# A hybrid decoder trunk's state-space scan: decay differences and six output gates on GpSimd, norm weights in the weight splits, z gates one step earlier

## What is computed

```python
zxbcdt = h @ w_in                                   # 1024 -> 2048 z, 3072 x/B/C, 32 dt
xbc = silu(causal_depthwise_conv(xbc, conv_w, conv_b))
a_cs = cumsum(dt * a)                               # per chunk of 128 tokens and head
decay = exp(where(causal, a_cs[l] - a_cs[s], -inf)) # 128 x 128 per head
y = (C B^T * decay) @ (x * dt) + (C @ state) * exp(a_cs) + d_skip * x
y = rms_norm(y * silu(z), norm_w)                   # norm_w: one weight per channel of 2048
x = x + g1 * (y @ w_out)                            # g1: the layer's output gate, from c
```

## Time and profile before

| | |
|---|---|
| median of 3 runs | 1495.35 us (1494.41 to 1498.49) |
| the profiled execution | 1497.73 us, its span 1495.9 us |
| PE busy, share of the span | 96% |
| DVE busy | 67% |
| ACT busy | 50% |
| POOL busy | 1% |
| granted PE clock | 0.991 |
| DMA, mean | 338 GB/s |

### The profile page before, as it was taken

How to read it: one execution, slowest core, us unless ns; L and a number is a source line. 1 busy time by engine, 2 the same in 40 slices (tenths; PEclk the granted TensorE clock), 3 DMA queues, 4 the chain that set the end, 5 groups by cost and what they waited for, 6 DMA issues and landing times.

```text
span 1495.9 us, 18527 instructions
## 1 busy us (share of the span) xinstructions
PE 1437.1 (96%) x6840; PEld 976.6 (65%) x6840; DVE 995.1 (67%) x1271; ACT 747.6 (50%) x977; POOL 18.6 (1%) x27
## 2 busy tenths in 40 slices
PE   7989999999999899999999999999999989999998
PEld 2835787888789778674666556756465655565573
DVE  2578788888659899764666646765654555655563
ACT  3565544444455896353446445644453444545361
POOL 0000000000000000000100000000000000000000
PEclk9999999999999999999999999999999999999999
DMA  9878698888366545679999999999999999999996
GB/s 361 330 248 292 240 396 303 301 295 301 103 217 185 162 161 204 261 288 409 364 412 406 411 374 416 418 420 420 409 420 413 420 420 418 413 420 414 420 419 247
DMA packets 118201, 506.01 MB, mean 338 GB/s; under 512 B 13779, under 2 KB 16492, under 8 KB 83032
## 3 DMA queue, kind: packets, MB, share of 16 engines
q1 hardware_dynamic: 115640, 496.51, 85.6%
q0 software_dynamic: 2464, 8.24, 1.6%
HBM read 502.52 MB, written 2.32 MB: 337 GB/s over the span
## 4 chain that ended last, share of the span: by engine, by line
PE 74%; DVE 10%; DMA 7%; ACT 6%; issue 3%; SPq 0%; DVEq 0%; ACTq 0%
PE acc L2685 16%; PE acc L2693 16%; PE acc L2686 16%; PE acc L3187 15%; DVE w_lo L1581 3%; ACT w_hi L1038 2%; DVE cv L2308 2%; DMA raw_rest<-in_moe_w_down 1%; DMA raw<-in_moe_w_down 1%; PE xb L3071 1%; DMA mod<-in_moe_w_gu 1%; PE acc L2834 1%; DMA mod<-in_moe_w_down 1%; DMA raw<-in_ada_w 1%; ACT dec L1487 1%
## 5 line engine op out<-in xcount | busy, mean ns | idle before, releaser
L1581 DVE TENSOR_TENSOR w_lo<-raw,w_hi 128x1024 fp32r<-128x1024 f32 x356 | 427.3, 1221 | 136.6 <-ACT w_hi L1038 126.1
L1038 ACT ACTIVATE w_hi<-raw 128x1024 fp32r<-128x1024 f32 x356 | 371.0, 1057 | 249.1 <-PE acc L2693 157.7
L2685 PE MATMUL acc<-w_hi,g_hi 128*128 128x512 f32 x448 | 179.3, 400 | 4.0 <-ACT w_hi L1038 3.9
L2686 PE MATMUL acc<-w_hi,g_lo 128*128 128x512 f32 x448 | 174.8, 390 | 0.0
L2685 PE MATMUL acc<-w_hi,a_hi 128*128 128x512 f32 x384 | 155.4, 405 | 8.5 <-ACT z_s L1404 7.7
L2686 PE MATMUL acc<-w_hi,a_lo 128*128 128x512 f32 x384 | 151.4, 394 | 0.0
L2693 PE MATMUL acc<-w_lo,g_hi 128*128 128x512 f32 x448 | 139.1, 392 | 4.1 <-DVE w_lo L1581 4.1
L3187 PE MATMUL acc<-raw,g_s 128*64 128x512 f32 x592 | 131.6, 594 | 0.5 <-DMA raw<-in_moe_w_gu 0.5
L2693 PE MATMUL acc<-w_lo,a_hi 128*128 128x512 f32 x384 | 119.5, 392 | 0.0
L1581 DVE TENSOR_TENSOR w_lo<-mod,w_hi 128x1024 fp32r<-128x1024 f32 x66 | 78.5, 1221 | 60.0 <-ACT w_hi L1038 58.2
L2685 PEld LDWEIGHTS acc<-w_hi,g_hi 128*128 128x128 f32 x448 | 84.2, 188 | 38.4 <-issue 12.7
(11 more groups left out here) (417 smaller groups left out, 2057.3 us busy)
## 6 DMA issues: line engine op xcount, KB each, us to landing
raw<-in_moe_w_gu SPq DMA_DIRECT2D x136, 1024.0 KB, 14.8
raw<-in_moe_w_down SPq DMA_DIRECT2D x66, 1024.0 KB, 16.5
raw<-in_ada_w SPq DMA_DIRECT2D x96, 512.0 KB, 6.0
mod<-in_moe_w_gu SPq DMA_DIRECT2D x40, 1024.0 KB, 13.8
raw<-in_ffn_w_gu SPq DMA_DIRECT2D x56, 512.0 KB, 5.9
mod<-in_moe_w_down SPq DMA_DIRECT2D x23, 1024.0 KB, 16.3
raw_more<-in_moe_w_gu SPq DMA_DIRECT2D x22, 1024.0 KB, 14.3
raw<-in_ssm_w_in SPq DMA_DIRECT2D x40, 512.0 KB, 5.0
```

Of the source, the lines that this page charges most:

```text
L1038: act.activation(w_hi[:, w % SPLIT, :], raw_tile(no), ACT.Copy).then_inc(hi_ready, 1)
L1581: dve.tensor_tensor(w_lo[:, w % SPLIT, :], raw_tile(no), r32(w_hi[:, w % SPLIT, :]), ALU.subtract).then_inc(raw_used, 1)
L2685: pe.matmul(o, l_hi[:, k, rows_], hi[:, col:col + HALF], start=new, stop=False)
L2686: pe.matmul(o, l_lo[:, k, rows_], hi[:, col:col + HALF], start=False, stop=False)
```

## The change

Three things are done.

1. **Decay differences on POOL.** POOL's loop over the units, which issued the loads of `acs_in`, now also computes the differences: eight `tensor_scalar` of 128x128 per unit, subtract and then minimum with 0. ACT's eight Relu go, and its Exp has no scale of -1 now. `acs_used` is set by POOL, and ACT waits for it.
2. **The output gate of six tiles on POOL.** After its differences of units 4, 5 and 6 POOL multiplies two `wout` tiles each by the gate row (`tensor_tensor`, 128x1024). DVE's `GATED_AT` goes. `y_gain` goes out of the gate and into the splits: for the 16 `wout` tiles ACT's split is an Identity with a scale per partition in place of a Copy, and DVE's a `scalar_tensor_tensor` in place of a `tensor_tensor`. DVE's ten other gates become `tensor_tensor`.
3. **z one step earlier.** `z_of_group(j)` stands at step `PROJ_END[Z0 + j] + 1`, that is 28, 32, 36 and 40, and ahead of the unit's Exp.

```diff
 def gated_no(stage, i):
-    return i + 1 + (KD if stage == "wout" else 0)
+    return i + 1 + (KD - GATED_AHEAD if stage == "wout" else 0)
...
 # ACT, split_hi
-act.activation(w_hi[:, w % SPLIT, :], raw_tile(no), ACT.Copy).then_inc(hi_ready, 1)
+if in_wout(no):
+    k = no - raw0["wout"]
+    act.activation(w_hi[:, w % SPLIT, :], raw_tile(no), ACT.Identity, scale=y_gain[:, k:k + 1]).then_inc(hi_ready, 1)
+else:
+    act.activation(w_hi[:, w % SPLIT, :], raw_tile(no), ACT.Copy).then_inc(hi_ready, 1)
...
 # ACT, gemm
-act.wait_ge(gated, gated_no(stage, i))
+if i < GATED_AHEAD:
+    act.wait_ge(gated_ahead, i + 1)
+else:
+    act.wait_ge(gated, gated_no(stage, i))
...
 # ACT, mixer_steps
+for j in range(SG):
+    if i == PROJ_END[Z0 + j] + 1:
+        z_of_group(j)
 for u in range(NU):
     if i == unit_in_at(u) + LEAD:
         unit_decays(u)
 if i in DECAYS_FIRST:
     conv_silu(i)
-for j in range(SG):
-    if i == PROJ_END[Z0 + j] + 2:
-        z_of_group(j)
...
 # ACT, unit_decays
 if u == 0:
     act.wait_ge(acs_ready, 1)
-if u >= 2:
-    act.wait_ge(acc_full, full_no(u - 2))
-act.wait_ge(ld_acs, 16 * (u + 1))
-for i in range(HG):
-    cols = slice(i * P, (i + 1) * P)
-    ins = act.activation(dec[:, u % 2, cols], acs_in[:, cols], ACT.Relu, scale=-1.0,
-                         bias=acs[:, c, HG * g + i:HG * g + i + 1])
-ins.then_inc(acs_used, 1)
+    act.activation(end_e[:, :, :], end_e[:, :, :], ACT.Exp).then_inc(acse_ready, 1)
 act.wait_ge(acs_used, u + 1)
-act.activation(dec[:, u % 2, :], dec[:, u % 2, :], ACT.Exp, scale=-1.0).then_inc(e_ready, 1)
+act.activation(dec[:, u % 2, :], dec[:, u % 2, :], ACT.Exp).then_inc(e_ready, 1)
...
 # DVE, split_lo
+if in_wout(no):
+    k = no - raw0["wout"]
+    dve.scalar_tensor_tensor(w_lo[:, w % SPLIT, :], raw_tile(no), y_gain[:, k:k + 1], r32(w_hi[:, w % SPLIT, :]),
+                             ALU.mult, ALU.subtract).then_inc(raw_used, 1)
...
 # DVE, gate_tile
-dve.scalar_tensor_tensor(tile, tile, y_gain[:, i:i + 1], mod[:, MOD_SLOT[1][2], :], ALU.mult, ALU.mult).then_inc(gated, 1)
+dve.tensor_tensor(tile, tile, mod[:, MOD_SLOT[1][2], :], ALU.mult).then_inc(gated, 1)
...
 # DVE, mixer_steps
-if i in GATED_AT:
-    gate_tile("wout", GATED_AT.index(i))
...
 # POOL, in the loop over the units, behind the DMA into acs_in
+if u == 0:
+    pool.wait_ge(acs_ready, 1)
+if u >= 2:
+    pool.wait_ge(acc_full, full_no(u - 2))
+pool.wait_ge(ld_acs, 16 * (u + 1))
+for i in range(HG):
+    cols = slice(i * P, (i + 1) * P)
+    ins = pool.tensor_scalar(dec[:, u % 2, cols], acs_in[:, cols], acs[:, c, HG * g + i:HG * g + i + 1], 0.0,
+                             ALU.subtract, ALU.min)
+ins.then_inc(acs_used, 1)
+for n in range((u - NU + 4) * 2, (u - NU + 5) * 2) if u >= NU - 4 and u < NU - 1 else ():
+    no = raw0["wout"] + n
+    pool.wait_ge(*raw_landed(no))
+    tile = raw_tile(no)
+    pool.tensor_tensor(tile, tile, mod[:, MOD_SLOT[1][2], :], ALU.mult).then_inc(gated_ahead, 1)
```

More of the change, by code:

```diff
@@ L329, in build @@
     acs_rows, st_acs, ld_acs, acs_used = (sem(n) for n in ("acs_rows", "st_acs", "ld_acs", "acs_used"))
+    gated_ahead = sem("gated_ahead")
     state_ready, e_ready, mt_ready, y_ready, yss_ready, yms_ready, yroot = (
@@ L495, in raw_landed, with in_wout @@
         return raw_ready[raw_sem[no]], 16 * raw_turn[no]
+    def in_wout(no):
+        return raw0["wout"] <= no < raw0["wout"] + 2 * KD
     def is_strip(no):
@@ L970, in home_free @@
                 elif name == "mod2":
+                    sp.wait_ge(gated_ahead, GATED_AHEAD)
                     sp.wait_ge(gated, gated_no("wout", 2 * KD - 1))
@@ L1481, in unit_decays @@
                     act.wait_ge(acs_ready, 1)
-                if u >= 2:
-                    act.wait_ge(acc_full, full_no(u - 2))
-                act.wait_ge(ld_acs, 16 * (u + 1))
-                for i in range(HG):
-                    cols = slice(i * P, (i + 1) * P)
-                    ins = act.activation(dec[:, u % 2, cols], acs_in[:, cols], ACT.Relu, scale=-1.0,
-                                         bias=acs[:, c, HG * g + i:HG * g + i + 1])
-                ins.then_inc(acs_used, 1)
+                    act.activation(end_e[:, :, :], end_e[:, :, :], ACT.Exp).then_inc(acse_ready, 1)
                 act.wait_ge(acs_used, u + 1)
-                if u == 0:
-                    act.activation(end_e[:, :, :], end_e[:, :, :], ACT.Exp).then_inc(acse_ready, 1)
-                act.activation(dec[:, u % 2, :], dec[:, u % 2, :], ACT.Exp, scale=-1.0).then_inc(e_ready, 1)
+                act.activation(dec[:, u % 2, :], dec[:, u % 2, :], ACT.Exp).then_inc(e_ready, 1)
                 if u == 0:
@@ L1580, in split_lo @@
                 dve.wait_ge(hi_ready, w + 1 + rep(e, BODY))
-                dve.tensor_tensor(w_lo[:, w % SPLIT, :], raw_tile(no), r32(w_hi[:, w % SPLIT, :]), ALU.subtract).then_inc(raw_used, 1)
+                if in_wout(no):
+                    k = no - raw0["wout"]
+                    dve.scalar_tensor_tensor(w_lo[:, w % SPLIT, :], raw_tile(no), y_gain[:, k:k + 1], r32(w_hi[:, w % SPLIT, :]),
+                                             ALU.mult, ALU.subtract).then_inc(raw_used, 1)
+                else:
+                    dve.tensor_tensor(w_lo[:, w % SPLIT, :], raw_tile(no), r32(w_hi[:, w % SPLIT, :]), ALU.subtract).then_inc(raw_used, 1)
             def gate_tile(stage, i):
@@ L2352, in y_turned @@
                 piece_lo(y_piece(q, t), tuple(part[q][:, :, t * P:(t + 1) * P] for part in (y_hi, y_lo)))
-            GATED_AT = (33, 35, 37, 39, 41, 43)
-            assert len(GATED_AT) == GATED_AHEAD
             def heads_of(row_, g):
```

## The result

| | before | changed |
|---|---|---|
| median | 1495.95 us of 4 runs (1494.41 to 1498.49) | 1514.43 us of 4 runs (1512.15 to 1517.16) |
| ratio | | 1.0123, 95% interval 1.0097 to 1.0148 |
| the profiled execution, its span | 1497.73, 1495.9 us | 1517.16, 1515.3 us |
| DVE, ACT, POOL busy | 67%, 50%, 1% | 66%, 48%, 6% |
| granted PE clock | 0.991 | 0.987 |

The change costs **18.5 us**; the forecast was +9.0. The direction was right; the size was half of what came, though the time lies inside the stated range.

A forecast was written before the change was run, and what follows sets the result against it. PE was taken to bound the stretch, paused by ACT's late silu(z), with DVE next. POOL's +20.5 us less z's 11.5 gave +9.0 us: 1506.7 against the profiled execution, 1504.4 us as median; range 1487 to 1518.

The forecast's parts named there:

- -11.5 for z: PE's waits for silu(z) at tiles 28 and 36, with the half clock after them, go: 11.5 us saved at most.
- +20.5 for what POOL takes from DVE: At tile 45, DVE loses 21.3 us to POOL, less 0.8 us of slack: 20.5 us late against unbroken PE.
- 17 us freer: ACT in the scan: 64 Relu, 19.5 us, go; two more function table changes of 1.28 us come; off the path.
- without interference: Tiles 33 and 45, POOL not slowing DVE: 11.5 less DVE's largest lateness, 5.1 at tile 33, gives 6.4 us faster.
- POOL's prices: Units 2 to 7: 48 differences at 0.305 us and six gates at 2.0, together 26.6 us; upper ends 0.61 and 2.56.
- If a POOL operation and such a DVE operation exclude each other: DVE operations reading two SBUF operands, 0.8 of the time, are blocked by POOL's 26.6 us: DVE loses 21.3 us.
- Rival B: POOL's load, differences and gates per unit reach tile 39 late at upper-end prices; 1495 to 1498 us, no change; chance 0.11.
- The signs named for the forecast's case and for B: Forecast's case: two-SBUF-input DVE operations over 1220 ns or gapped while POOL computes; B: ACT's Exp waiting for POOL from unit 5.
- Rival A: Tiles 28 to 45: POOL works beside DVE freely, price 0; 1489.0 us; chance 0.33.
- Rival C: z still late behind ACT's Exp waiting for POOL; PE's pauses only change place; 1495 us; chance 0.07.
- The splits: 16 wout tiles: scale in ACT's split costs nothing; DVE's low splits +0.9 us, cancelled by ten other gates at -0.6.
- What follows passes the loss on: Behind wout, a microsecond saved or lost carries over to the kernel's end as one.

The follow-up runs named there:

- e1: Kernel before with only silu(z) one step earlier and ahead of the Exp; 1500.19 us, ratio 1.0028.
- e6: e1 with seven Relu of eight left out from unit 2 on; from POOL's dt store to DVE's first operation behind wout 167.3 us, whole time not comparable.
- e2: e1 plus six gates on POOL with the gains in the splits, ACT keeping its Relu; 1506.05 us, ratio 1.0065.
- e8: e1 with POOL's differences and products run by themselves at program start, DVE having nothing to do; one run took 1500.86 us.
- e13: e1 with each unit's eight differences shared, heads 0 to 3 on ACT and 4 to 7 on POOL; 1495.97 us, ratio 1.0007.
- e3: e1 plus all decay differences on POOL with whole loads, DVE keeping its gates; 1504.58 us, ratio 1.0066.

## Why the prediction was right and wrong

The sum had two terms, -11.5 for z and +20.5 for what POOL takes from DVE. Measured were +3.9 (e1) and +14.5 (the changed kernel above e1; its two parts by themselves make 14.7). The step that failed is the first, and in the second the path of the differences.

- **"PE's two pauses should go: -11.5 us if nothing else is late."** The pauses went, the 11.5 us did not come: z moved alone costs 3.9 us of the stretch (e1), 15.4 off. The condition was examined for DVE alone. ACT's queue was taken to be "17 us freer", but what stands behind z and the Exp on ACT was not asked: the copy that frees the transposes' bank, whose lateness the pause for z had hidden. With seven of eight Relu left out as well the gain is 3.1 us (e6, DVE keeping its gates), where 6.4 was forecast "without interference".
- **POOL's prices.** Taken were 0.305 and 2.0 us; the runs show 0.69 and 2.39 for POOL alone, and 0.95 and 2.80 beside DVE. Units 2 to 7 took POOL 43.0 + 16.7 = 59.7 us where the forecast had 26.6 and its upper end 44.6. The difference was priced by ACT's row, the engine it left, and its upper end by nothing but a factor. The text asked which prices would break it and looked only downward.
- **"If a POOL operation and such a DVE operation exclude each other, DVE loses 0.8 x 26.6."** For the gates that is right: DVE lost 13.3 us to 14.1 us of gates in e2. Beside the differences it is POOL that loses, 0.69 us becoming 0.95 to 1.21, which lengthens POOL's chain. The forecast said that each "also waits for DVE's", and gave it no price.
- **Rival B, POOL's own chain, had 0.11 and sets the end.** It was worked as if instead of the port, and from unit 4 on time; but at 13.0 us a unit POOL is already late at unit 4 (525.71 us, not 518.0). Its own formula with the measured end, 580.9 - 554.1 - 11.5, gives +15.3 of the +18.4. The signs named for the forecast's case and for B stood side by side: longer DVE operations beside the gates, and an Exp that waits for POOL, 29.3 us from unit 2 on.
- **Rival A** is out: DVE is blocked by the gates. **Rival C** was right that the pauses change place, but no wait for z is left, and its +-0 was 3.9 us too kind.
- **The splits** cost what was taken or little more: the low one 1280 ns against 1278, ACT's with a scale 1150 ns against 1053, the 0.1 us a tile that the text allowed for.
- **What follows passes the loss on** was right: 878.9 us behind the stretch against 877.7.

The sum missed by 9.4 us of the stretch: z came out 15.4 above the forecast, POOL's part 6.0 below. That it still had the right sign is partly luck: a loss from the port that was too large for the differences stood in for a chain that was left out.

## What to carry to other kernels

Before work goes to an engine that sits idle, work out that engine's own loop, with its transfers and issues in line and at prices measured on that engine, and hold it against the period of the engine that sets the pace. At the prices that POOL has alone (e8), with 0.3 us ahead of the issue and 4.4 from issue to landing, a unit is 5.55 + 0.3 + 4.4 = 10.3 us against 8.8 without gates and 15.0 with two: POOL falls behind before any port is asked about. When a wait is taken away by moving work forward on a queue, list what is behind it on that queue and who waits there. Half the work moved can cost nothing where all of it costs (ratio 1.0007 in e13, 1.0066 in e3), but here it gained nothing over the kernel before either.

## What the runs showed of the hardware

- A `tensor_scalar` of POOL with a scalar from SBUF and two operations took 0.69 us for 128x128 and 3.75 us for 128x1024 alone, longer than its `tensor_tensor` of two 128x1024 tiles, 2.39. The Trainium skill (GPSIMD Engine Reference, § 4.1) calls one-input work on GpSimd roughly line rate; this form is not, DVE's two-operand operation on that size taking 1.22.
- Who lost when a DVE operation with two SBUF operands met one of POOL depended on the POOL operation. DVE's stood still for two gates in a row in e2 (4.41, 5.22 and 5.77 us for 0.7). The last of them had started 0.49 us ahead of the gates, but while POOL issued a load (546.38 us, 0.59 us long); which of the two held it is not shown. Beside differences DVE's kept its time but for 0.15 us in e3, and POOL's took up to 2.64 us for 0.71, and 0.95 to 1.21 on average over the runs.
- A load of 512 KB over all partitions issued by POOL took 3.7 to 4.6 us in the chain; in halves it was hidden, but each issue held POOL 0.6 us, behind 0.3 us of wait for its last difference.
